# Attention scores as row-tiled products: 64-row products in both row halves, 32-row products in four strips, value products in one run a slot

## What is computed

```python
def bidir_attention(q, k, v):          # 6 heads, 96 wide: 64 plain + 32 rotary; v 64 wide
    def one_block(q_blk):
        s = jnp.einsum('bqhd,bkhd->bhqk', q_blk, kf) * scale
        p = jax.nn.softmax(s, axis=-1)
        return jnp.einsum('bhqk,bkhd->bqhd', p, v)
```

## Time and profile before

| | |
|---|---|
| median of 3 runs | 5518.92 us (5514.96 to 5520.15) |
| the profiled execution's own time | 5531.59 us |
| its span, first to last instruction | 5529.7 us |
| granted TensorE clock, mean of the span | 0.976 |
| PE busy (matmuls) | 5253.9 us, 95% |
| DVE, ACT, POOL busy | 2836.4, 2069.1, 641.7 us |
| score products (L1701), busy | 745.6 us in 1632 halves |
| transposes of probabilities (L1708), busy | 479.2 us in 3264 |
| value products (L1724), busy | 411.2 us in 1536 and 25.9 us in 96 halves |

### The profile page before, as it was taken

One profiled execution on the slowest core, in us unless ns is written; L12 is line 12 of the kernel. 1 busy time (PEld: TensorE's weight loads), 2 busy tenths in 40 slices (PEclk: granted clock), 3 DMA queues, 4 the chain that ended last, 5 costly groups with the idle time before them and its releaser, 6 DMA issues. The chain is left out here.

```text
span 5529.7 us, 94771 instructions
## 1 busy us (share of the span) xinstructions
PE 5253.9 (95%) x38844; PEld 2827.2 (51%) x38844; DVE 2836.4 (51%) x4438; ACT 2069.1 (37%) x3470; POOL 641.7 (12%) x1110
## 2 busy tenths in 40 slices
PE   8999999999979999989989999998999799999899
PEld 3444444478764444444444444444778644444454
DVE  2221486555545555556522214766555455555565
ACT  1211555245544444421112115552455444444211
POOL 0000000044430000001100000000444200000011
PEclk9999999999999999999999999999999899999999
DMA  5311565456550111026343115654655501110253
GB/s 223 138 69 59 187 211 181 154 158 162 144 147 11 35 38 25 5 106 223 121 160 138 67 68 172 211 188 158 160 158 147 146 7 37 36 25 5 98 176 119
DMA packets 570089, 646.07 MB, mean 117 GB/s; under 512 B 228336, under 2 KB 455152, under 8 KB 559872
## 3 DMA queue, kind: packets, MB, share of 16 engines
q1 hardware_dynamic: 569072, 638.88, 36.8%
q10 hardware_dynamic: 592, 1.15, 0.1%
HBM read 372.77 MB, written 267.13 MB: 116 GB/s over the span
## 5 line engine op out<-in xcount | busy, mean ns | idle before, releaser
L490 PE MATMUL ps<-feat_hT,w_features 128*128 128x512 f32 x2240 | 972.5, 592 | 0.0
L808 PE MATMUL ps<-w_tokens,prep_hT 128*128 128x512 f32 (+1 forms) x1920 | 827.0, 591 | 22.9 <-DMA prep_hT<-s_ht 22.9
L1701 PE MATMUL ps<-att_K,att_Q 96*128 96x512 f32 x1632 | 745.6, 600 | 32.5 <-DMA att_K<-s_qkt 22.8
L490 PEld LDWEIGHTS ps<-feat_hT,w_features 128*128 128x128 f32 x2240 | 420.4, 190 | 505.9 <-issue 503.2
L1815 DVE TENSOR_REDUCE att_mx<-ps 128x1 f32<-128x1024 f32 x384 | 470.3, 1225 | 286.4 <-PE ps L1701 286.4
L808 PEld LDWEIGHTS ps<-w_tokens,prep_hT 128*128 128x128 f32 x1920 | 365.8, 192 | 475.8 <-issue 450.2
L1708 PEld LDWEIGHTS ps<-kc,att_pr 128*128 128x128 f32 x3264 | 362.8, 141 | 433.0 <-issue 319.1
L2096 PE MATMUL ps<-w_out,fin_yT 128*128 128x512 f32 x1280 | 569.3, 598 | 2.5 <-DVE fin_yT L2046 2.5
L1779 ACT ACTIVATE att_PT<-ps 128x512 f32<-128x512 f32 x384 | 228.0, 594 | 691.2 <-PE ps L1708 691.0
L1708 PE MATMUL ps<-kc,att_pr 128*128 128x128 f32 x3264 | 479.2, 279 | 5.3 <-DVE att_PT L1824 2.5
L1701 PEld LDWEIGHTS ps<-att_K,att_Q 96*128 96x128 f32 x1632 | 297.2, 192 | 336.0 <-issue 257.9
(11 more groups left out here) (226 smaller groups left out, 6783.6 us busy)
## 6 DMA issues: line engine op xcount, KB each, us to landing
s_sc<-prep_sc SPq DMA_DIRECT2D x20, 3072.0 KB, 9.2
scan_src<-s_sc SPq DMA_DIRECT2D x160, 384.0 KB, 4.8
s_qkt<-scan_qT SPq DMA_DIRECT2D x40, 576.0 KB, 4.1
fin_z<-s_zt SPq DMA_DIRECT2D x40, 576.0 KB, 5.3
s_zf<-feat_co SPq DMA_DIRECT2D x88, 256.0 KB, 2.5
s_ht<-feat_hT SPq DMA_DIRECT2D x10, 2048.0 KB, 7.9
prep_hT<-s_ht SPq DMA_DIRECT2D x40, 512.0 KB, 5.6
s_zt<-prep_st SPq DMA_DIRECT2D x80, 256.0 KB, 3.6
```

The source lines that it names most:

```text
L490: last = pe.matmul(b, wf[:, k, i * P:(i + 1) * P], hT[g % 2][:, k, :], start=(k == 0), stop=(k == KD - 1))
L808: last = pe.matmul(ps[:, tiles.bank(pieces[n]), 0:c1 - c0], hT[j % NH][:, k, :], wt[:, k, c0:c1], start=(k == 0), stop=(k == KD - 1))
L1701: pe.matmul(ps[:, c, :], Q[:, t * P:(t + 1) * P], K[:, k0:k0 + G], start=True, stop=True).then_inc(scored, 1)
```

## The change

- The queries and keys of a head lie in one tile 128 partitions wide instead of two of 96: the 64 plain rows of the queries twice (partitions 0 to 63 and 64 to 127), their 32 rotary rows four times. The long sequence's keys are spread: the plain rows of keys 0 to 1023 in the upper half and of 1024 to 2047 in the lower, the rotary rows of each 512 keys in a strip of 32 partitions of its own. The short sequence's keys are copied like the queries.
- Every score product of 96 rows becomes one of 64 rows and one of 32 rows that add up in the same bank. A slot makes two 64-row products (banks 0 and 1, one in each half of the rows), four 32-row products (banks 0 to 3, one in each strip), and two 64-row products (banks 2 and 3). The wait for the second pair of banks to come free stands ahead of the third 32-row product. The first two banks are reported done with their 32-row products.
- Bank c holds the key block 0, 2, 1, 3 (`KEYS`); `weigh` picks the values to match.
- Both value pairs of a slot follow each other, between the second and the third quarter's transposes.
- ACT makes both exponentials of a slot before it copies the third quarter.
- A head is loaded by six DMAs instead of two (its first one in parts). The tile of even heads is that of `w_out`, whose load moves from the start of the stage to after the scores of head 4.

```diff
+    HALF = (slice(0, DN), slice(DN, P))
+    KEYS = (0, 2, 1, 3)
+    LAST_IN_WO = HB - 2 + HB % 2
...
-        Qs = [sb(f"Q{b}", [DQK, T]) for b in range(2)]
-        Ks = [sb(f"K{b}", [DQK, T]) for b in range(2)]
+        heads_in = (late[0][:, :, :].rearrange("p k n -> p (k n)"), sb("qk", [P, 2 * T + 2 * T0 + 3 * G])[:, :])
+        Q_N, Q_R, K_N, K_R = 0, T, 2 * T, 2 * T + T0 + 2 * G
...
+                def load_queries(h, c0, c1, sem):
+                    w, rows = heads_in[h % 2], d["qkt"][h * DQK:(h + 1) * DQK, c0:c1]
+                    sp.dma_start(w[:, Q_N + c0:Q_N + c1], rows[0:DN, :].unsqueeze(0).to_broadcast([2, DN, c1 - c0])).then_inc(sem, 16)
+                    sp.dma_start(w[:, Q_R + c0:Q_R + c1], rows[DN:DQK, :].unsqueeze(0).to_broadcast([4, DR, c1 - c0])).then_inc(sem, 16)
...
-                load_qk(0, 0, T0, first_in)
-                load_qk(0, T0, T, arrived[0])
+                load_queries(0, 0, T0, first_in)
+                load_first_keys(0, first_in)
+                load_queries(0, T0, T, arrived[0])
+                load_keys(0, arrived[0])
                 load_v(0)
-                load_qk(1, 0, T, arrived[1])
+                load_head(1, arrived[1])
                 load_v(1)
                 wo, ws, ln = late
-                sp.dma_start(wo[:, :, :], d["w_out"][:, l * KD:(l + 1) * KD, :]).then_inc(late_in, 16)
...
+                    if h == LAST_IN_WO:
+                        sp.wait_ge(scored, 4 * NSLOT * (h + 1))
+                        sp.dma_start(wo[:, :, :], d["w_out"][:, l * KD:(l + 1) * KD, :]).then_inc(late_in, 16)
...
-                    for c in range(4):
+                    def freed(c):
                         if n:
                             pe.wait_ge(exps, exp_count[n - 1][c])
-                        t, k0 = (c, 0) if s == 0 else (TPG - 1 + s, T0 + c * G)
-                        pe.matmul(ps[:, c, :], Q[:, t * P:(t + 1) * P], K[:, k0:k0 + G], start=True, stop=True).then_inc(scored, 1)
+                    def rows64(c):
+                        t, k0 = (c, 0) if s == 0 else (TPG - 1 + s, T0 + G * (KEYS[c] % 2))
+                        q, k = w[HALF[c % 2], Q_N + t * P:Q_N + (t + 1) * P], w[HALF[c % 2], K_N + k0:K_N + k0 + G]
+                        return pe.matmul(ps[:, c, :], q, k, start=(c < 2), stop=(c >= 2))
+                    def rows32(c):
+                        t, k0 = (c, 0) if s == 0 else (TPG - 1 + s, T0)
+                        r = slice(DR * KEYS[c], DR * (KEYS[c] + 1))
+                        return pe.matmul(ps[:, c, :], w[r, Q_R + t * P:Q_R + (t + 1) * P], w[r, K_R + k0:K_R + k0 + G], start=(c >= 2), stop=(c < 2))
+                    for c in range(2):
+                        freed(c)
+                        rows64(c)
+                    for c in range(4):
+                        if c >= 2:
+                            freed(c)
+                        last = rows32(c)
+                        if c < 2:
+                            last.then_inc(scored, 1)
+                    for c in range(2, 4):
+                        rows64(c).then_inc(scored, 1)
...
-                    for u in now[0:1]:
+                    if turns:
+                        turn(n - 1, 1)
+                    for u in now:
                         weigh(*u)
                     if turns:
-                        turn(n - 1, 1)
                         turn(n - 1, 2)
-                    for u in now[1:2]:
-                        weigh(*u)
-                    if turns:
                         turn(n - 1, 3)
...
                     if n < NS:
                         exponentials(n, 0)
+                    if n < NS:
+                        exponentials(n, 1)
                     if turns:
                         turned_out(n - 1, 2)
-                    if n < NS:
-                        exponentials(n, 1)
```

More of the change, by code:

```diff
@@ new lines, in load_first_keys, with load_keys @@
+                def load_first_keys(h, sem):
+                    w, rows = heads_in[h % 2], d["qkt"][(HB + h) * DQK:(HB + h + 1) * DQK, 0:T0]
+                    sp.dma_start(w[:, K_N:K_N + T0], rows[0:DN, :].unsqueeze(0).to_broadcast([2, DN, T0])).then_inc(sem, 16)
+                    sp.dma_start(w[:, K_R:K_R + T0], rows[DN:DQK, :].unsqueeze(0).to_broadcast([4, DR, T0])).then_inc(sem, 16)
+                def load_keys(h, sem):
+                    w, rows = heads_in[h % 2], d["qkt"][(HB + h) * DQK:(HB + h + 1) * DQK, T0:T]
+                    sp.dma_start(w[:, K_N + T0:K_R], rows[0:DN, :].rearrange("r (b c) -> b r c", b=2)).then_inc(sem, 16)
+                    sp.dma_start(w[:, K_R + T0:K_R + T0 + G], rows[DN:DQK, :].rearrange("r (b c) -> b r c", b=4)).then_inc(sem, 16)
@@ L1664, in load_v, with load_head @@
+                def load_head(h, sem):
+                    load_queries(h, 0, T, sem)
+                    load_first_keys(h, sem)
+                    load_keys(h, sem)
                 def load_v(h):
                     sp.dma_start(Vs[h % 2][:, :, :], d["va"].rearrange("(n p) c -> p n c", p=P)[:, :, h * (DV + 1):(h + 1) * (DV + 1)]).then_inc(v_in[h % 2], 16)
-                load_qk(0, 0, T0, first_in)
-                load_qk(0, T0, T, arrived[0])
+                load_queries(0, 0, T0, first_in)
@@ L1679, in _ @@
                         sp.wait_ge(summed, GROUPS * (h + 1))
-                        load_qk(h + 2, 0, T, arrived[h % 2])
+                        load_head(h + 2, arrived[h % 2])
                         load_v(h + 2)
+                    if h == LAST_IN_WO:
+                        sp.wait_ge(scored, 4 * NSLOT * (h + 1))
+                        sp.dma_start(wo[:, :, :], d["w_out"][:, l * KD:(l + 1) * KD, :]).then_inc(late_in, 16)
                     sp.wait_ge(normed, GROUPS * (h + 1))
@@ L1691, in scores @@
                     h, s = slots[n]
-                    Q, K = Qs[h % 2], Ks[h % 2]
+                    w = heads_in[h % 2]
                     if h == 0 and s == 0:
-                        pe.wait_ge(first_in, 32)
+                        pe.wait_ge(first_in, 64)
                     elif s == (1 if h == 0 else 0):
-                        pe.wait_ge(arrived[h % 2], 32 * (h // 2 + 1))
-                    for c in range(4):
+                        pe.wait_ge(arrived[h % 2], 96 * (h // 2 + 1) - (32 if h % 2 == 0 else 0))
+                    def freed(c):
                         if n:
                             pe.wait_ge(exps, exp_count[n - 1][c])
-                        t, k0 = (c, 0) if s == 0 else (TPG - 1 + s, T0 + c * G)
-                        pe.matmul(ps[:, c, :], Q[:, t * P:(t + 1) * P], K[:, k0:k0 + G], start=True, stop=True).then_inc(scored, 1)
+                    def rows64(c):
[17 more added lines that the diff above has]
+                        rows64(c).then_inc(scored, 1)
                 def turn(n, x):
@@ L1723, in weigh @@
                         kb = 2 * i + half
-                        last = pe.matmul(ps[DV * half:DV * half + DV, BANK_O, :], V[:, kb + (TPG if k else 0), 0:DV], PT[:, kb, :],
+                        last = pe.matmul(ps[DV * half:DV * half + DV, BANK_O, :], V[:, TPG + TPG * KEYS[kb // TPG] + kb % TPG if k else kb, 0:DV], PT[:, kb, :],
                                          start=(i == 0), stop=final_pair((g, i)))
```

## The result

| | before | changed |
|---|---|---|
| median of 4 runs beside each other, us | 5519.5 (5515.0 to 5524.6) | 5559.7 (5554.5 to 5561.7) |
| ratio, 95% interval | 1 | 1.0071 [1.0054, 1.0089] |
| span of the profiled execution, us | 5529.7 | 5559.0 |

A forecast was written before the change was run, and what follows sets the result against it. PE, 95% busy, was taken as the bound; -80.6 (slots) + 5 (heads' first slots) - 2.4 (early slots) + 7 (loads) = -71.0 gave 5448 us against the median of 5518.9. Range 5425 to 5490, to 5512 with the first rival.

The forecast's parts named there:

- Loads: Start of each attention stage: larger query and key loads at 243 GB/s cost 3.5 us a layer, +7 in all.
- copying a row several times drops it to 160: Start of the attention stage: worse case of a load rate falling to 160 GB/s, costing 12 us a layer.
- The slot: Ordinary attention slot on PE: 7.09 us instead of 7.51, 0.42 less, 80.6 us less over 192 slots.
- A head's second slot: Slot after each head's first: waits 0.25 us at the second bank and 0.25 at the fourth, +5 us over ten.
- Slots without value products: Slots of 6.51 us, taken as bound by the chain to the exponentials: gain about 0.1 us each.
- Strips only partly together: Score strips on PE: weight loads in turn give 5512 us, a 1.12 us round near 5498; chance 0.12.
- strips in pairs: Score strips on PE: only two under way at once, block 0.86 us more, slot 7.95, 5616 us; chance 0.10.
- estimated round of 1.12 us: Four strip products on PE, by the skill's 3.07 times: 1.12 us instead of 0.86, time near 5498 us.
- The chain becomes the bound: Attention slots: semaphores over 0.8 us late keep slots above 7.09; 5486 us at 0.2 beyond slack; folded into forecast's width.
- the early slots' gain: The 12 early slots of the attention stages: 0.2 us less each, -2.4 us.

The follow-up runs named there:

- e1_split: The changed kernel with each copy of a row block loaded by a DMA of its own, 18 loads a head instead of 6: 5464.9 us, ratio 0.9902.
- e6_loads_ordered: e1_split with head 0 loaded in order of need, ACT issuing its first keys and the later queries coming last: 5455.8 us, ratio 0.9891.
- e2_run_only: The kernel before with only both value pairs in one run and ACT's two exponentials side by side; scores and loads as before: 5466.0 us, ratio 0.9904.
- e5_packed_two_runs: e1_split with the value products back in two runs and ACT's copy back between the exponentials: 5524.9 us, ratio 1.0013 against the kernel before.
- e7_strips_first: e1_split with all four 32-row strip products ahead of the four 64-row products, two row-tiled blocks a slot instead of three: 5488.6 us, ratio 0.9950.
- e3_lead2: The kernel before with the source of its query and key loads written with an outermost dimension of 2, same bytes: 5577.2 us, ratio 1.0104.
- e8_lead4: The kernel before with the source of its query and key loads written with an outermost dimension of 4: 5539.6 us in one run beside 5519.8.
- e4_lead16: The kernel before with the source of its query and key loads written with an outermost dimension of 16: 5515.5 us in one run beside 5517.5.

## Why the prediction was wrong

**The step that failed is the one headed "Loads".** It multiplied bytes by the queue's 243 GB/s of the earlier trace rows. That rate belongs to loads of 96 rows; a load with a leading 2 runs at 52 and one with a leading 4 at 105. By the earlier trace rows the first 1.05 MB were to come 2.6 us late, and were 15.8 late in the first layer; the second slot was to come 3.5 late, and was 56.4 late (52.4 in the second layer). The bounds failed too: "copying a row several times drops it to 160" was a guess at another mechanism that no row supports, and allowed 12 us a layer where 54 came. The trace of before has a leading 2 only on transfers of 4 KB, which show no rate, so the far bound should have been one engine of sixteen. The Trainium skill's rule, cited above, gives the engines outright; it speaks against this change, and the prediction did not weigh it.

**The same step by its own mechanism was also too low.** With all engines in use (e1_split) the start costs 7.7 and 6.8 us a layer up to the second slot, not 3.5. Ordered better (e6_loads_ordered) it costs 4.2 and 2.4.

**The slot was right.** 7.10 against the forecast 7.09, with three equal blocks of 1.06. Of it 0.30 comes from the merged run (e2_run_only) and 0.10 from the packed scores (e5_packed_two_runs; forecast 0.11). A head's second slot loses 0.50, as forecast. Slots without value products gain 0.34 (6.17 against 6.51) instead of 0.1. There the prediction had named the wrong bound, the chain to the exponentials. Before, with the start at 1664.52 and the next at 1671.03:

```profile
1668.06 1.04 PE L1708 MATMUL ps<-kc,att_pr 128*128 128x128 f32 x8
...
1670.48 0.63 PE L1708 MATMUL ps<-kc,att_pr 128*128 128x128 f32 x4 [0.41 <-DVE att_PT L1824]
```

and in the changed kernel, where the next slot starts at 1718.92:

```profile
1712.75 1.13 PE L1730 MATMUL ps<-w_out 64*128 64x512 f32 x4
...
1715.96 1.09 PE L1754 MATMUL ps<-kc,att_pr 128*128 128x128 f32 x8
...
1718.36 0.63 PE L1754 MATMUL ps<-kc,att_pr 128*128 128x128 f32 x4 [0.34 <-DVE att_PT L1868]
```

The score blocks take 3.21 instead of 3.54. The transposes behind them wait for the copies out of their own two banks and take 2.96 instead of 2.97, so what the scores save shows in full.

**The rivals.** "Strips only partly together" and "strips in pairs" both fell: the four strip products start at 1798.074, .081, .087 and .094, and their block costs 1.07. The estimated round of 1.12 us that the prediction worked out from the Trainium skill's 3.07 times is not seen here: with it the block would have cost 1.32. Against the 3.44 of four products in a row the whole block is 3.2 times as fast, with an entering and leaving of 0.20 that a block of two halves pays as well. "The chain becomes the bound" fell for this order and holds for that of e7_strips_first. The slower outcome came by a mechanism that was on no list.

**By its sum.** Attention stages: forecast -71, measured +34.5, apart by 105.5. The starts make up 104 of it (108.4 against 7 - 2.4, since this sum puts all the early slots' gain there), the slots 2 (-73.9 against -75.6). The rest of the distance to the median, some 6 us, lies outside these stages or between runs and was not traced.

## What to carry to other kernels

Price a load by its form before its bytes: look at the outermost dimension (it was small on the source side in the runs here; the Trainium skill's rule cited above counts the tile's side too, which no run here shows), and write a replicated tile as one load per copy, so that the rows come outermost. A load's slowness is hidden in the steady state and paid in full where a stage starts; here that was two slots of 102. When a change has two parts, price each by itself: merging the value products gave 0.96% with a few moved lines. Packing the scores added nothing to that until its loads were split and reordered, and then 10 us of the attention stages (1494.9 in e2_run_only, 1484.9 in e6_loads_ordered), which the medians show too, with overlapping intervals.

## What was not expected of the hardware

- The DMA rate follows the outermost dimension: 52 GB/s and 2.1 busy engines with 2, 105 and 4.0 with 4, 226 and all engines with 16, for the same bytes from the same rows.
- One engine alone moves more when few are in use: a packet of 8192 bytes takes 0.31 us, 26 GB/s, in the windows of e3_lead2 and e8_lead4, and 0.52 us, 16 GB/s, in that of e4_lead16. The loss from sixteen engines to two is 226 / 52 = 4.3 times here, not 8.
- Four fp32 products of 32 rows by 512 columns on four strips take a block of 1.07 us, no longer than two of 64 rows on two halves (1.06), switches included.
